# Expert retrieval by row gathers, replaced by dense products over all experts with a gate table in DRAM

## The chip, the cores and the metric

The kernel runs on one core of a Trainium2 chip. The metric is the device time of one execution in microseconds. Everything is fp32.

## What is computed

The reference is one decoder layer on 1024 tokens of width 1024: attention of two kinds, an output projection, then a channel mixer that retrieves experts. The change is in the mixer:

```python
s1, s2 = q[:, :, 0] . keys1, q[:, :, 1] . keys2      # per token, 8 heads, 128 keys on each side
v1, i1 = top_k(s1, 16);  v2, i2 = top_k(s2, 16)
top_s, pos = top_k(all 256 sums v1 + v2, 16)
idx  = i1 * 128 + i2 of those 16                     # one of 16384 experts
gate = softmax(top_s)
h    = gelu(x2[token] . u[idx])                      # u, v: 16384 x 1024
out[token] = x1[token] + sum over 8 x 16 picks of gate * h * v[idx]
```

So each token uses 128 of the 16384 rows of u and of v. A last rmsnorm with a gain follows.

## The kernel before

The 1024 tokens are 8 tiles of 128, one token to a partition. The stages run one after another with barriers between: `project`, `stick`, `window` and `mix` (attention, output projection; `mix` leaves x1 and the normed x2 in DRAM and x2 transposed in SBUF as `x2_t`), then `experts`.

`experts` begins with the key scores (class `KeyScores`, L796 to L894). A unit is one of 16 half-heads by some tiles: 8 matmuls give the queries (L874), ScalarE copies them (L847), one matmul of 128 columns a tile gives the scores (L884), ScalarE copies those out (L856). The first pass does tiles 0 and 1 (16 units of 256 columns), the second tiles 2 to 7 (32 units, of 512 and 256 columns in turn). Scores go to DRAM.

Routing runs on VectorE (L1103 to L1189): two rounds of the eight largest on each half-head, a table of 256 sums a head, two rounds again, then a comparison with a ramp that looks up the keys' numbers. Every step waits for the one before. ScalarE does the exponential (L1316).

Then, for each tile, 128 picks in groups of 8. GpSimd issues for every pick one gather of 128 rows of 4 KB, one for each token, from u or from v (L1063):

```python
nc.gpsimd.indirect_dma_start(
    out=ring[:, k, :], out_offset=None, in_=table,
    in_offset=bass.IndirectOffsetOnAxis(ap=stage[:, half, k:k + 1], axis=0)).then_inc(full[k], 16)
```

VectorE multiplies the gathered rows of u with x2 and sums (L1197). The gelu is put together from an exponential on ScalarE and small VectorE operations (`weigh`). ScalarE turns each pick's weight into a diagonal matrix (L1335), and TensorE adds diagonal times gathered rows of v in PSUM, two matmuls of 512 columns a pick (L1372). The gathers of v of tile t and of u of tile t+1 alternate on GpSimd's queue, each behind a ring of 8 buffers. In the last tile VectorE takes one pick of eight from TensorE (`extra`, L1221). `finish` (L1233) adds x1, norms and hands the tile to SP's queue.

What sets the order is written out by hand: each engine runs its own program, and semaphores with counts tie them. SP's queue carries loads and stores that are not gathers, in program order, and a wait in it holds up what is behind it.

## Time and profile before

| | us |
|---|---|
| median of 3 runs | 4058.27 (4055.64 to 4059.77) |
| span of the profiled execution | 4053.9 |
| TensorE busy (matmul) | 2946.8 (73%) |
| VectorE busy | 2097.3 (52%) |
| ScalarE busy | 704.7 (17%) |
| GpSimd busy | 2393.8 (59%) |
| DMA, mean over the span | 1153.17 MB, 284 GB/s |

The profile is of one execution; its span runs from the first instruction to the last, and the execution times of the runs include what lies around it. An engine's busy share is an average over stages that have different limits, so it has to be read by stretches. In a group of instructions the first number behind the bar is the time in which at least one of them ran, the second the mean duration of one; matmuls are pipelined, so their durations overlap.

### The profile page before, as it was taken

Reading aid. Unit: us, or ns where it says so; the run is one execution under the profiler, and the core shown is the slowest. Engines: PE = TensorE matmul, PEld = TensorE weight load, DVE = VectorE, ACT = ScalarE, POOL = GpSimd, SP = SyncE. Lnnn points to the kernel's source line nnn. Section 1 sums busy time; section 2 is a strip of 40 time slices with the busy share of each in tenths; the row PEclk is TensorE's granted clock in tenths of the full one; section 3 lists DMA queues with packets and bytes.
Section 4 is the critical chain, followed back from the end, with each engine's and each line's share of the span. In section 5 each row is a group of like instructions: output and inputs, shape, how many; then the busy total and the mean of one; then the engine's idle time right before and its main releaser. Section 6 shows DMA issues by size and latency. Waiting matters only on the chain.

```text
span 4053.9 us, 36202 instructions
## 1 busy us (share of the span) xinstructions
PE 2946.8 (73%) x8280; PEld 1429.7 (35%) x8280; DVE 2097.3 (52%) x4538; ACT 704.7 (17%) x1566; POOL 2393.8 (59%) x2391
## 2 busy tenths in 40 slices
PE   8998978899056776666666676666766667666699
PEld 4655564566022232222222232222322223222243
DVE  1007872258856555654665465556645654444411
ACT  1116632111011111111111111111111111111122
POOL 1001004116777777777777777777777777777765
PEclk8999999999577888778887887878888788888899
DMA  3000012558899999999999999999999999999998
GB/s 104 32 0 1 1 47 85 166 167 298 286 369 324 358 370 348 347 348 360 354 357 346 370 345 348 353 374 334 353 351 381 335 343 356 365 354 356 354 334 304
DMA packets 352122, 1153.17 MB, mean 284 GB/s; under 512 B 36240, under 2 KB 80272, under 8 KB 351120
## 3 DMA queue, kind: packets, MB, share of 16 engines
q0 software_dynamic: 294912, 1073.87, 71.6%
q1 hardware_dynamic: 57104, 78.14, 5.6%
q8 instruction: 36, 0.59, 0.1%
q14 instruction: 70, 0.57, 0.0%
HBM read 1130.90 MB, written 20.97 MB: 284 GB/s over the span
## 4 chain that ended last, share of the span: by engine, by line
issue 27%; POOL 27%; PE 12%; DVE 8%; DMA 6%; POOLq 2%; DVEq 0%; ACT 0%; another core or an unknown queue 0%; SPq 0%; ACTq 0%
POOL ex_u L1063 14%; POOL ex_v L1063 11%; PE ex_acc L1372 10%; DMA ex_u<-in_peer_u,ex_index_u 4%; DMA ex_v<-in_peer_v,ex_index_v 2%; DVE ex_prod L1197 2%; PE kl_q L874 2%; DVE bias L1197 1%; POOL ex_index_v L1055 1%; DVE ex_left L1115 1%; DVE ex_half_i L1114 1%; POOLq L993 1%; DVE ex_half_v L1111 1%; POOLq L994 1%; POOL ex_index_u L1055 0%
## 5 line engine op out<-in xcount | busy, mean ns | idle before, releaser
L1372 PE MATMUL ex_acc<-ex_v,ex_diag 128*128 128x512 f32 x4032 | 2017.0, 664 | 1007.4 <-DMA ex_v<-in_peer_v,ex_index_v 768.5
L1372 PEld LDWEIGHTS ex_acc<-ex_v,ex_diag 128*128 128x128 f32 x4032 | 854.8, 215 | 2168.9 <-issue 2160.9
L1063 POOL DMA_INDIRECT ex_u<-in_peer_u,ex_index_u x1024 | 1114.3, 1088 | 385.4 <-issue 318.5
L1063 POOL DMA_INDIRECT ex_v<-in_peer_v,ex_index_v x1024 | 1066.7, 1042 | 414.5 <-issue 306.2
L1197 DVE CUSTOM_DVE_ANT_0 ex_prod<-ex_u,ex_x 128x1024 f32<-128x1024 f32 x512 | 628.7, 1228 | 1008.7 <-DMA ex_u<-in_peer_u,ex_index_u 878.2
L1335 ACT ACTIVATE ex_diag<-ident,ex_wt 128x128 f32<-128x128 f32 x1008 | 398.1, 401 | 2242.4 <-PE ex_acc L1372 1517.9
L1197 DVE CUSTOM_DVE_ANT_0 bias<-ex_u,ex_x 128x1024 f32<-128x1024 f32 x512 | 628.8, 1228 | 80.6 <-DMA ex_u<-in_peer_u,ex_index_u 53.2
L874 PE MATMUL kl_q<-x_t,ex_v 128*128 128x256 f32 (+1 forms) x768 | 228.3, 450 | 0.8 <-DVE keys_t L1254 0.8
L468 POOL TENSOR_SCALAR_AFFINE_SELECT st_sp<-st_sp 128x1024 f32<-128x1024 f32 x8 | 8.7, 1090 | 362.4 <-DVE st_sp L422 362.4
L252 PE MATMUL pj_acc<-x_t,pj_w 128*128 128x512 f32 x384 | 167.4, 599 | 1.3 <-DVE x_t L207 1.3
L874 PEld LDWEIGHTS kl_q<-x_t,ex_v 128*128 128x128 f32 x768 | 142.3, 190 | 66.4 <-issue 53.6
L415 DVE SCALAR_TENSOR_TENSOR x_t<-st_zs 128x1024 f32<-128x1024 f32 x36 | 45.4, 1262 | 142.6 <-ACT st_zs L371 142.4
L775 PE MATMUL mx_y<-qk_t,mx_mt 128*128 128x512 f32 x256 | 114.4, 605 | 3.7 <-ACT mx_mt L706 3.7
L252 PEld LDWEIGHTS pj_acc<-x_t,pj_w 128*128 128x128 f32 x384 | 73.7, 192 | 94.0 <-issue 92.3
L754 POOL TENSOR_TENSOR mx_hs<-mx_hs,minus_half 128x16 f32<-128x16 f32 x8 | 23.2, 2905 | 137.3 <-DMA mx_g<-in_norm_g 131.1
L325 PE MATMUL st_c<-st_sp,tri 128*128 128x512 f32 x144 | 79.4, 644 | 9.3 <-POOL st_sp L468 8.1
L1197 DVE DVE_READ_ACCUMULATOR2_ANT ex_dots<- 128x1 f32 x1024 | 84.1, 82 | 0.0
L1068 POOL TENSOR_TENSOR ex_index_ut<-ex_index,ex_zero_i 128x128 int32<-128x128 int32 x8 | 7.8, 979 | 126.7 <-DVEq L1189 124.3
L224 DVE COPY pj_w_twice<-pj_w 128x1024 f32<-128x1024 f32 x2 | 1.3, 690 | 145.9 <-DMA pj_w<-in_w_in 145.9
L775 PEld LDWEIGHTS mx_y<-qk_t,mx_mt 128*128 128x128 f32 x256 | 48.9, 194 | 64.5 <-issue 58.8
L249 PE MATMUL pj_acc<-pj_w,x_t 128*128 128x256 f32 (+1 forms) x384 | 69.9, 344 | 0.0
L1055 POOL TENSOR_TENSOR ex_index_v<-ex_index_vt,ex_zero_i 128x8 int32<-128x8 int32 x128 | 60.2, 470 | 11.9 <-PE ex_acc L1372 5.7
(162 smaller groups left out, 1930.2 us busy)
## 6 DMA issues: line engine op xcount, KB each, us to landing
ex_v<-in_peer_w_q SPq DMA_DIRECT2D x16, 1024.0 KB, 5.8
ex_u<-in_peer_u,ex_index_u POOLq DMA_INDIRECT x1024
ex_v<-in_peer_v,ex_index_v POOLq DMA_INDIRECT x1024
pj_w<-in_w_in SPq DMA_DIRECT2D x9, 1024.0 KB, 5.8
x_scratch<-mx_x SPq DMA_DIRECT2D x16, 512.0 KB, 2.7
ex_x<-x_scratch SPq DMA_DIRECT2D x16, 512.0 KB
ex_sc<-score_scratch SPq DMA_DIRECT2D x7, 1024.0 KB
mixed<-in_x SPq DMA_DIRECT2D x8, 512.0 KB, 4.1
```

Of the source, the lines that this page charges most:

```text
L249: last = nc.tensor.matmul(acc[:, n % 4, 0:at[1]], h_t[:, c, part * P:(part + 1) * P], slot[:, c, at[0]:at[0] + at[1]], **st)
L252: last = nc.tensor.matmul(acc[:, n % 4, :], slot[:, c, at:at + P], h_t[:, c, part * HALF:(part + 1) * HALF], **st)
L325: last = nc.tensor.matmul(csum[:, cols], tri[:], soft[:, n % 3, cols], start=True, stop=kb == i)
L415: nc.vector.scalar_tensor_tensor(out=lsp[:, n % 2, :], in0=zs[:, n % 4, :], scalar=-1.0, in1=zs[:, n % 4, :], op0=ALU.mult, op1=ALU.max).t ...
L775: last = nc.tensor.matmul(y[:, t % 2, hf * HALF:(hf + 1) * HALF], m_t[:, t % 2, c, :], w[:, c, hf * HALF:(hf + 1) * HALF], start=c == 0, s ...
L874: last = self.nc.tensor.matmul(self.q[:, n % 2, 0:tiles * P], self.w[:, g % self.ring, c, (b % 2) * P:(b % 2 + 1) * P], self.x2_t[:, c, fi ...
L993: engine.wait_ge(signal, value)
L1055: nc.gpsimd.tensor_tensor(stage[:, half, :], tile_index[:, bass.ds(j * RG, RG)], zero_i[:, 0:RG], ALU.add).then_inc(ready, 1)
L1063: nc.gpsimd.indirect_dma_start(out=ring[:, k, :], out_offset=None, in_=table, in_offset=bass.IndirectOffsetOnAxis(ap=stage[:, half, k:k + ...
L1197: nc.vector.tensor_tensor_reduce(out=prod[k % 2][:], in0=u[:, k, :], in1=x2[:], scale=1.0, scalar=0.0, op0=ALU.mult, op1=ALU.add, accum_ou ...
L1335: nc.scalar.activation(diag[:, k, :], ident[:], ACT.Copy, scale=wt[:, bass.ds(j * RG + k, 1)]).then_inc(diag_ready, 1)
L1372: ins = nc.tensor.matmul(acc[:, hf * HALF:(hf + 1) * HALF], diag[:, k, :], v[:, k, hf * HALF:(hf + 1) * HALF], start=first and k == 0, sto ...
```

## The change

`experts` is rewritten; the stages before it stay, but for `mix`, which no longer stores x2. Nothing is gathered. The 16384 experts are 128 chunks of 128. The tiles form three teams, [0, 1], [2, 3, 4] and [5, 6, 7], and each team passes over all chunks. For one chunk and one team (an iteration, 384 in all):

- SP loads the chunk of u (laid out transposed on the host, 512 KB) and of v (512 KB), each into a ring of 4 (`load_u`, `load_v`).
- TensorE: `hidden(k)`, 8 matmuls with the team's columns of `x2_t` as the moving side, gives expert x token products in the PSUM bank `hp`.
- ScalarE: `gelu(k)` with the built-in function. VectorE: `gated(k)` multiplies with the chunk's gates.
- TensorE: `values(k)` multiplies with v and adds in PSUM, for each tile of the team two matmuls of 512 columns.

The gates of a tile are a table of 128 chunks x 128 experts x 128 tokens that is zero but for the picks. It is made in 32 batches of 4 tokens: VectorE makes two one-hot matrices, picks by keys (`one_hots`), one of them weighted with the gates; TensorE multiplies them, one matmul of 128 columns a token (`build`), into the PSUM bank `gp`; ScalarE copies it with a turn of the axes (`read_gates`) to a staging buffer, and after 32 tokens SP stores 2 MB to DRAM (`store_gates`). SP loads them back in blocks of 8 chunks (`load_gates`). Both move in runs of 1 KB.

Tiles 0 and 1 are routed and their tables made before the loop. For tiles 2 to 7 the routing, cut into 61 pieces, and the batches are spread over the iterations of team 0 and team 1 by the tables `ROUTES`, `TURNS` and `BUILDS`; team 2 has neither. All loops are unrolled.

The core of the diff:

```diff
+CHUNKS = 128
+TEAMS = [[0, 1], [2, 3, 4], [5, 6, 7]]
+RING = 4
+SUB = 32
+BATCH = 4
+BLOCK = 8
...
+    ROUTES = {0: [(2, 0, 3), (3, 21, 2), (4, 53, 2), (5, 86, 2)], 1: [(6, 0, 2), (7, 32, 2)], 2: []}
+    TURNS = {0: {22: 2, 56: 3, 90: 4, 125: 5}, 1: {33: 6, 67: 7}, 2: {}}
+    BUILDS = {0: [(2, 24), (3, 58), (4, 92)], 1: [(5, 0), (6, 35), (7, 69)], 2: []}
+    PIECES = 61
...
+                def load_u(k):
+                    if k >= RING:
+                        sp.wait_ge(h_ready, k - RING + 1)
+                    sp.dma_start(u[:, k % RING, :, :], peer_ut[k % CHUNKS]).then_inc(u_in[k % RING], 16)
+                def load_v(k):
+                    if k >= RING:
+                        sp.wait_ge(v_done, k - RING + 1)
+                    sp.dma_start(v[:, k % RING, :], v_view[k % CHUNKS]).then_inc(v_in[k % RING], 16)
+                def load_gates(n):
+                    team = TEAMS[n // BLOCKS]
+                    if n >= 2:
+                        sp.wait_ge(a_ready, BLOCK * (n - 1))
+                    if n % BLOCKS == 0:
+                        for s in range(2):
+                            sp.wait_ge(gates_stored[s], 16 * (SUBS // 2) * (team[-1] + 1))
+                    subs = len(team) * SUBS
+                    sp.dma_start(gb[:, n % 2, 0:subs, :],
+                                 gate_dram[team[0] * SUBS:team[0] * SUBS + subs, n % BLOCKS].rearrange(
+                                     "s p f -> p s f")).then_inc(gb_in[n % 2], 16)
+                def store_gates(t, q):
+                    s = t * SUBS + q
+                    sp.wait_ge(gp_read, first_use(t) + 1 + (q + 1) * SUB // BATCH)
+                    sp.dma_start(gate_dram[s].rearrange("k p f -> p k f"),
+                                 stage[:, s % 2, :, :].rearrange("p (k c) t -> p k (c t)", c=BLOCK)).then_inc(
+                                     gates_stored[s % 2], 16)
...
+                for k in range(RING):
+                    load_u(k)
+                    load_v(k)
+                for n in range(UNITS):
                     ks.store(sp, n)
-                    if n == SIDES + 8:
+                    if n == SIDES + 12:
                         load_scores(1)
                 ks.all_stored(sp)
-                load_scores(2)
-                load_x2(1)
-                with sp.Fori(1, TILES - 2) as t:
-                    load_scores(t + 2)
-                    load_x2(t + 1)
-                    turn_over(t)
-                load_x2(TILES - 1)
-                turn_over(TILES - 2)
-                turn_over(TILES - 1)
-                sp.wait_ge(y_done, TILES)
-                sp.dma_start(out_v[TILES - 1], y[:]).then_inc(stored, 16)
+                sp.wait_ge(ks.s_ready, UNITS)
+                for t in TEAMS[0]:
+                    for q in range(SUBS):
+                        store_gates(t, q)
+                    if t == 0:
+                        load_scores(2)
+                load_gates(0)
+                load_gates(1)
+                for k in range(TOTAL):
+                    l, c = k // CHUNKS, k % CHUNKS
+                    if k + RING < TOTAL:
+                        load_u(k + RING)
+                    if RING <= k + RING - 1 < TOTAL:
+                        load_v(k + RING - 1)
+                    if c % BLOCK == 2 and c > BLOCK and c // BLOCK + 1 < BLOCKS:
+                        load_gates(l * BLOCKS + c // BLOCK + 1)
+                    if k >= 1 and (done := built_at(k - 1)) and (done[1] + 1) % (SUB // BATCH) == 0:
+                        store_gates(done[0], done[1] // (SUB // BATCH))
+                    for t, first, rate in ROUTES[l]:
+                        if c == first + 20 // rate + 3 and t + 1 < TILES:
+                            load_scores(t + 1)
+                    if l >= 1:
+                        for j, t in enumerate(TEAMS[l - 1]):
+                            if c == j + 8:
+                                store_out(t, j)
+                    if c == 60:
+                        load_x1(l)
+                    if c == CHUNKS - 1 and l + 1 < len(TEAMS):
+                        load_gates((l + 1) * BLOCKS)
+                        load_gates((l + 1) * BLOCKS + 1)
...
+                def one_hots(t, i):
+                    b = t * (P // BATCH) + i
+                    if i == 0:
+                        dve.wait_ge(gp_read, first_use(t) + 1)
+                    if b >= 2:
+                        dve.wait_ge(gp_full, first_use((b - 2) // (P // BATCH)) + 2 + (b - 2) % (P // BATCH))
+                    cols = slice(i * BATCH, (i + 1) * BATCH)
+                    nc.vector.tensor_tensor(oh[:, b % 2, 0, :, :], bcast(iota[:].unsqueeze(1), [P, BATCH, NK]),
+                                            bcast(tr[:, t % 2, 1, cols].unsqueeze(2), [P, BATCH, NK]), ALU.is_equal)
+                    for j in range(BATCH):
+                        n = i * BATCH + j
+                        last = nc.vector.tensor_scalar(oh[:, b % 2, 1, j, :], iota[:], tr[:, t % 2, 0, n:n + 1],
+                                                       tr[:, t % 2, 2, n:n + 1], ALU.is_equal, ALU.mult)
+                    last.then_inc(oh_ready, 1)
+                def gated(k):
+                    team, c = team_of(k), k % CHUNKS
+                    block = k // BLOCK
+                    subs, width = len(team) * SUBS, len(team) * P
+                    dve.wait_ge(gelu_done, k + 1)
+                    dve.wait_ge(gb_in[block % 2], 16 * (block // 2 + 1))
+                    if k >= 2:
+                        dve.wait_ge(v_done, k - 1)
+                    at = c % BLOCK * SUB
+                    nc.vector.tensor_tensor(a[:, k % 2, 0:width].rearrange("p (s t) -> p s t", t=SUB),
+                                            act_h[:, k % 2, 0:width].rearrange("p (s t) -> p s t", t=SUB),
+                                            gb[:, block % 2, 0:subs, at:at + SUB], ALU.mult).then_inc(a_ready, 1)
...
+                gated(0)
+                for k in range(TOTAL):
+                    l, c = k // CHUNKS, k % CHUNKS
+                    if l >= 1:
+                        if c == 0:
+                            for j in range(len(TEAMS[l - 1])):
+                                add_rows(l - 1, j)
+                    if k + 1 < TOTAL:
+                        gated(k + 1)
+                    if l >= 1:
+                        for j, t in enumerate(TEAMS[l - 1]):
+                            if c == j + 3:
+                                mean(t)
+                            if c == j + 5:
+                                scale_rows(t, j)
+                    if k + 1 < TOTAL and (batch := built_at(k + 1)):
+                        one_hots(*batch)
+                    if what := routed_at(k):
+                        for n in range(what[1], what[2]):
+                            route(what[0], n)
+                l = len(TEAMS) - 1
+                for j in range(len(TEAMS[l])):
+                    add_rows(l, j)
+                for t in TEAMS[l]:
+                    mean(t)
+                for j, t in enumerate(TEAMS[l]):
+                    scale_rows(t, j)
...
+                def read_gates(t, i):
+                    s = t * SUBS + i * BATCH // SUB
+                    act.wait_ge(gp_full, first_use(t) + 2 + i)
+                    if i * BATCH % SUB == 0 and s >= 2:
+                        act.wait_ge(gates_stored[s % 2], 16 * (s // 2))
+                    at = i * BATCH % SUB
+                    nc.scalar.activation(stage[:, s % 2, :, at:at + BATCH], gp[:].rearrange("p t n -> p n t"),
+                                         ACT.Copy).then_inc(gp_read, 1)
+                def gelu(k):
+                    width = len(team_of(k)) * P
+                    act.wait_ge(h_ready, k + 1)
+                    if k >= 2:
+                        act.wait_ge(a_ready, k - 1)
+                    nc.scalar.activation(act_h[:, k % 2, 0:width], hp[:, 0:width], ACT.Gelu_apprx_tanh).then_inc(gelu_done, 1)
...
+                def build(t, i):
+                    b = t * (P // BATCH) + i
+                    pe.wait_ge(oh_ready, b + 1)
+                    pe.wait_ge(gp_read, first_use(t) + 1 + i)
+                    for j in range(BATCH):
+                        last = nc.tensor.matmul(gp[:, j, :], oh[:, b % 2, 0, j, :], oh[:, b % 2, 1, j, :], start=True, stop=True)
+                    last.then_inc(gp_full, 1)
+                def hidden(k):
+                    team = team_of(k)
+                    first, width = team[0] * P, len(team) * P
+                    pe.wait_ge(u_in[k % RING], 16 * (k // RING + 1))
+                    if k >= 1:
+                        pe.wait_ge(gelu_done, k)
+                    for j in range(CH):
+                        last = nc.tensor.matmul(hp[:, 0:width], u[:, k % RING, j, :], x2_t[:, j, first:first + width],
+                                                start=j == 0, stop=j == CH - 1)
+                    last.then_inc(h_ready, 1)
...
+                def values(k):
+                    team, c = team_of(k), k % CHUNKS
+                    pe.wait_ge(v_in[k % RING], 16 * (k // RING + 1))
+                    pe.wait_ge(a_ready, k + 1)
+                    for j, t in enumerate(team):
+                        if c == 0 and k >= 1 and j < len(team_of(k - 1)):
+                            pe.wait_ge(y_ready, team_of(k - 1)[j] + 1)
                         for hf in range(2):
+                            last = nc.tensor.matmul(acc[:, j, hf * HALF:(hf + 1) * HALF], a[:, k % 2, j * P:(j + 1) * P],
+                                                    v[:, k % RING, hf * HALF:(hf + 1) * HALF],
+                                                    start=c == 0, stop=c == CHUNKS - 1)
+                    last.then_inc(v_done, 1)
...
+                for t in TEAMS[0]:
+                    turn_picks(t)
+                    for i in range(P // BATCH):
+                        build(t, i)
+                hidden(0)
+                pe.wait_ge(ks.s_read, UNITS)
+                for k in range(TOTAL):
+                    if k + 1 < TOTAL:
+                        hidden(k + 1)
+                    if (t := turned_at(k)) is not None:
+                        turn_picks(t)
+                    values(k)
+                    if batch := built_at(k):
+                        build(*batch)
...
+        if name == "peer_u":
+            a = _np.ascontiguousarray(a.reshape(CHUNKS, P, CH, P).transpose(0, 3, 2, 1))
```

`route` does what the old `pick_` functions did, piece by piece. `add_rows`, `mean` and `scale_rows` finish a tile; GpSimd only takes the power of the mean square. The ring of w_q in the key scoring has 3 slots where it had 4 (they lie in `gb` now), and the exponential of tile 0 is asked of ScalarE behind unit 26, where it was behind unit 18.

## Rows read from the trace of the kernel before

**Rows 1.** The stretches: us, then busy time of each engine, clock, DMA share, GB/s
```profile
core 0: us, PE busy (x) PEld busy (x) DVE busy (x) ACT busy (x) POOL busy (x), PEclk, DMA share, GB/s
...
0.00:770.00 770.00, 680.33 (x3225) 400.37 (x3225) 304.14 (x378) 245.66 (x398) 99.80 (x71) 0.95 0.13 45
770.00:1020.00 250.00, 249.47 (x1024) 174.49 (x1024) 161.28 (x538) 44.15 (x112) 85.24 (x75) 1.00 0.70 235
1020.00:4054.00 3034.00, 2016.97 (x4032) 854.80 (x4032) 1631.91 (x3624) 414.92 (x1057) 2208.75 (x2246) 0.82 0.94 349
```

**Rows 2.** The page, part 3: DMA queues (packets, MB, share of 16 engines)
```profile
q0 software_dynamic: 294912, 1073.87, 71.6%
q1 hardware_dynamic: 57104, 78.14, 5.6%
```

**Rows 3.** Groups by line and form: busy, mean ns | idle before, releasers
```profile
L1372 PE MATMUL ex_acc<-ex_v,ex_diag 128*128 128x512 f32 x4032 | 2017.0, 664 | 1007.4 <-DMA ex_v<-in_peer_v,ex_index_v 768.5 <-ACT ex_diag L1335 142.6 <-issue 96.2
...
L1063 POOL DMA_INDIRECT ex_u<-in_peer_u,ex_index_u x1024 | 1114.3, 1088 | 385.4 <-issue 318.5 <-POOL ex_index_u L1055 60.8 <-DVE ex_dots L1197 4.0
...
L874 PE MATMUL kl_q<-x_t,ex_v 128*128 128x256 f32 x512 | 115.7, 379 | 0.8 <-DVE keys_t L1254 0.8
```

**Rows 4.** TensorE in order of time, key scoring: start, us, line, operands
```profile
777.43 3.62 PE L874 MATMUL kl_q<-x_t,ex_v 128*128 128x256 f32 x16
780.89 0.61 PE L884 MATMUL kl_s<-keys_t,kl_qt 128*128 128x128 f32 x4
...
832.03 7.03 PE L874 MATMUL kl_q<-x_t,ex_v 128*128 128x512 f32 x16
838.90 0.61 PE L884 MATMUL kl_s<-keys_t,kl_qt 128*128 128x128 f32 x4
...
842.80 1.05 PE L884 MATMUL kl_s<-keys_t,kl_qt 128*128 128x128 f32 x8
843.69 6.60 PE L874 MATMUL kl_q<-x_t,ex_v 128*128 128x512 f32 x15
```

**Rows 5.** TensorE in order of time, the last tile
```profile
3848.80 195.49 PE L1372 MATMUL ex_acc<-ex_v,ex_diag 128*128 128x512 f32 x448 [15.95 <-ACT ex_diag L1335]
```

**Rows 6.** Two stretches, TensorE alone: us, busy, clock, DMA share, GB/s
```profile
3000.00:3500.00 500.00, 333.49 (x656) 0.82 0.95 356
3850.00:4044.00 194.00, 194.00 (x447) 0.99 0.92 333
```

**Rows 7.** Groups by form, ScalarE, VectorE and GpSimd
```profile
L856 ACT ACTIVATE kl_out<-kl_s 128x512 f32<-128x512 f32 x16 | 9.6, 597 | 8.3 <-PE kl_s L884 6.3 <-issue 2.0
...
L1129 DVE TENSOR_TENSOR ex_cand<-ex_half_v 128x256 f32<-128x256 f32 x64 | 22.3, 420 | 1.7 <-DVE ex_half_f L1127 0.8
...
L759 POOL TENSOR_TENSOR mx_rs<-mx_rs,minus_half 128x1 f32<-128x1 f32 x8 | 4.4, 556 | 55.4 <-DVE mx_rs L741 55.4
```

**Rows 8.** VectorE in order of time, routing of tile 0
```profile
849.66 2.04 DVE L1140 MAX8 ex_best<-ex_cand 128x8 f32<-128x256 f32 x6
...
864.66 0.23 DVE L1156 TENSOR_SCALAR ex_part_i<-ex_pos 128x128 uint32<-128x128 uint32 x1
...
883.10 0.29 DVE L1186 TENSOR_TENSOR ex_gates<-ex_gate_e,ex_gsum 128x128 f32<-128x128 f32 x1
```

**Rows 9.** ScalarE in order of time, end of key scoring
```profile
1019.55 0.87 ACT L856 ACTIVATE kl_out<-kl_s 128x512 f32<-128x512 f32 x2 [0.51 <-PE kl_s L884]
```

**Rows 10.** DMA issues: KB each, median us to landing
```profile
ex_v<-in_peer_w_q SPq DMA_DIRECT2D x16, 1024.0 KB, 5.8
...
x_scratch<-mx_x SPq DMA_DIRECT2D x16, 512.0 KB, 2.7
```

**Rows 11.** Everything in order of time, the end
```profile
4044.38 1.23 DVE L1239 TENSOR_TENSOR ex_y<-ex_acc,bias 128x1024 f32<-128x1024 f32 x1 [2.12 <-PE ex_acc L1372]
4045.64 1.03 ACT L1324 ACTIVATE ex_ysq<-ex_y 128x1024 f32<-128x1024 f32 x1 [12.83 <-DVE ex_y L1239]
...
4050.87 0.34 SPq L1040 DMA_DIRECT2D out<-ex_y  x1
```

More of the change, by code:

```diff
@@ L893, in multiply, with experts, team_of, built_at @@
             self.score(pe, n)
-def experts(nc, sem, ident, spare, keys_t, keys1, keys2, w_q, x2_t, score_dram, x1_dram, x2_dram, peer_u, peer_v, final_g, out):
-    RG = 8
-    GROUPS = PICKS // RG
+def experts(nc, sem, ident, minus_half, keys_t, keys1, keys2, w_q, x2_t, score_dram, gate_dram, x1_dram, peer_ut, peer_v,
+            final_g, out):
     score_t = score_dram.rearrange("(t p) n -> t p n", p=P)
     x1_v = x1_dram.rearrange("(t p) n -> t p n", p=P)
-    x2_v = x2_dram.rearrange("(t p) n -> t p n", p=P)
     out_v = out.rearrange("(t p) n -> t p n", p=P)
+    v_view = peer_v.rearrange("(c p) d -> c p d", p=P)
+    TOTAL = len(TEAMS) * CHUNKS
+    SUBS = P // SUB
+    USES = P // BATCH + 1
+    BLOCKS = CHUNKS // BLOCK
+    MOST = max(len(team) for team in TEAMS)
+    ROUTES = {0: [(2, 0, 3), (3, 21, 2), (4, 53, 2), (5, 86, 2)], 1: [(6, 0, 2), (7, 32, 2)], 2: []}
+    TURNS = {0: {22: 2, 56: 3, 90: 4, 125: 5}, 1: {33: 6, 67: 7}, 2: {}}
+    BUILDS = {0: [(2, 24), (3, 58), (4, 92)], 1: [(5, 0), (6, 35), (7, 69)], 2: []}
+    PIECES = 61
+    def team_of(k):
+        return TEAMS[k // CHUNKS]
+    def built_at(k):
+        for t, first in BUILDS[k // CHUNKS]:
+            if first <= k % CHUNKS < first + P // BATCH:
+                return t, k % CHUNKS - first
+        return None
+    def turned_at(k):
+        return TURNS[k // CHUNKS].get(k % CHUNKS)
+    def routed_at(k):
+        for t, first, rate in ROUTES[k // CHUNKS]:
+            n = (k % CHUNKS - first) * rate
+            if 0 <= n < PIECES:
+                return t, n, min(PIECES, n + rate)
+        return None
     with ExitStack() as ctx:
@@ L1067, in copy_index @@
-                def copy_index(dest, source, value):
-                    nc.gpsimd.tensor_tensor(dest[:], source[:], zero_i[:], ALU.add).then_inc(index_moved, 1)
-                    hold(pool, index_moved, value)
-                pool.wait_ge(picked, 1)
-                copy_index(index_ut, index, 1)
-                with pool.Fori(0, GROUPS // 2) as pair:
-                    for half in range(2):
-                        gathers(0, 2 * pair + half, half, peer_u, u, index_ut, index_u, u_full, u_free, iu_ready)
@@ L1086, in _ @@
-                copy_index(index_vt, index_ut, 2 * TILES)
-                with pool.Fori(0, GROUPS // 2) as pair:
-                    for half in range(2):
-                        gathers(TILES - 1, 2 * pair + half, half, peer_v, v, index_vt, index_v, v_full, v_free, iv_ready,
-                                RG - 1)
+                nc.gpsimd.iota(iota_i[:], pattern=[[1, NK]], base=0, channel_multiplier=0).then_inc(setup, 1)
+                for t in range(TILES):
+                    pool.wait_ge(mean_done, t + 1)
+                    nc.gpsimd.tensor_tensor(fs[:, 2, t:t + 1], fs[:, 1, t:t + 1], minus_half[:, 0:1],
+                                            ALU.pow).then_inc(rstd_done, 1)
@@ new lines, in _ @@
+                gelu(0)
+                for k in range(TOTAL):
+                    l, c = k // CHUNKS, k % CHUNKS
+                    if k + 1 < TOTAL:
+                        gelu(k + 1)
+                    if (t := turned_at(k)) is not None:
+                        read_turned(t)
+                    if batch := built_at(k):
+                        read_gates(*batch)
+                    for t, first, rate in ROUTES[l]:
+                        if c == first + 39 // rate + 2:
+                            gate_exp(t)
+                    if l >= 1:
+                        for j, t in enumerate(TEAMS[l - 1]):
+                            if c == j + 1:
+                                square(t, j)
@@ L1364, in _ @@
+                for j, t in enumerate(TEAMS[-1]):
+                    square(t, j)
             @block.tensor
             def _(pe):
-                def group(t, j, first, last, slots):
-                    at = t * PICKS + j * slots
-                    for k in range(slots):
-                        pe.wait_ge(v_full[k], 16 * (t * GROUPS + j + 1))
-                        pe.wait_ge(diag_ready, at + k + 1)
-                        for hf in range(2):
-                            ins = nc.tensor.matmul(acc[:, hf * HALF:(hf + 1) * HALF], diag[:, k, :],
-                                                   v[:, k, hf * HALF:(hf + 1) * HALF],
-                                                   start=first and k == 0, stop=last and k == slots - 1)
-                        ins.then_inc(v_free, 1)
@@ L1377, in tile, with turn_picks @@
-                def tile(t, slots=RG):
-                    group(t, 0, True, False, slots)
-                    with pe.Fori(1, GROUPS - 1) as j:
-                        group(t, j, False, False, slots)
-                    group(t, GROUPS - 1, False, True, slots)
+                def turn_picks(t):
+                    pe.wait_ge(picked, t + 1)
+                    if t >= 1:
+                        pe.wait_ge(gp_read, first_use(t))
+                    for j in range(3):
+                        last = nc.tensor.transpose(gp[:, j, :], row[:, j, :], ident[:])
+                    last.then_inc(gp_full, 1)
```

549 lines of the change are left out of this document (201 added, 348 removed).

## The prediction, made before the changed kernel had run

> **What bounds the kernel now.** Read the stretches first [rows 1]: 770 us of attention and mixing, 250 us of key scoring with TensorE full at 249.5 us, then 3034 us of experts. In the last, the 16 DMA engines are busy 0.94 of the time at 349 GB/s, TensorE 2017 of 3034 us, VectorE 1632. The DMA table [rows 2] names the traffic: 1073.87 MB of gathered rows of u and v. The groups by line [rows 3] show who waits for it: TensorE's 4032 records of L1372 sat idle 1007 us, 769 of them for a gather of v. GpSimd is close behind: 1.09 us for a gather of u [rows 3], those of v alike, 2209 us busy in the stretch [rows 1]. So the expert stage is a DMA stage with a third of TensorE free. The last row of [rows 3] settles how a matmul is to be counted: 32 units of 8 matmuls of 256 columns stand as x512. Each fp32 matmul of the program is two records. A 512-column record takes 195.49/448 = 0.436 us in a dense run [rows 5], so a matmul takes about twice that.
>
> **What goes.** All gathers, GpSimd's work, the 1024 products of 1.23 us on VectorE, the diagonals on ScalarE, 16 stores of x2 and 8 loads of it: the DMA bound ends. In return every token meets every one of 16384 experts.
>
> **TensorE's new work, the term that decides.** Key scoring already runs the three shapes, back to back with full cover [rows 4]. Eight matmuls of 256 columns: 780.89-777.43 = 3.46 us. Eight of 512: 838.90-832.03 = 6.87 us, or 0.859 each. Four of 128: 843.69-842.80 = 0.89 us. Eight of 384, by interpolation between the first two: 5.165 us (the cost is linear in columns, 1.68 ns each).
> - A team of two tiles, one chunk of 128 experts: `hidden` is 8x256, 3.46 us; `values` is 4x512, 3.44 us; 6.90 us. Times 128: 883 us.
> - A team of three: 8x384 is 5.165, 6x512 is 5.15; 10.32 us. Times 256 for two teams: 2641 us.
> - Gate tables of tiles 2 to 7, inside the loop: 6x32 batches of 4 matmuls of 128 columns, 0.89 us: 171 us. Six turns of 3 transposes: 4 us.
> Sum of the loop: 3699 us of TensorE that nothing hides, since it is TensorE itself, against the 3034 us of the whole old stage. The old stage used 2016 matmuls there, the new one 6144 times two shapes; trading 1 us of gather for dense products costs more products than DMA gave back.
>
> **What lies beside it.** Each iteration is 7.8 us (team of two with a batch) to 11.2 us.
> - ScalarE: the gelu from PSUM, 256 or 384 columns, up to the 0.60 us of 512 columns [rows 7], and the read of four gate tables, 512 columns, 0.60 us. 1.2 of 7.8. The single `hp` buffer makes `hidden(k+1)` wait for `gelu(k)`, but `values(k-1)`, 3.4 us, stands between.
> - VectorE: `gated`, 384 columns at the 1.2 ns a column of the 1024-column sum (1.23 us in [rows 11]), 0.46. One-hots of a batch: a 512-column compare, 0.70 (twice 22.3/64 [rows 7]), and four of 128 columns at 0.23 [rows 8], 0.9. Routing: 37 pieces of tile 0 took 849.66 to 883.39 [rows 8], 0.92 us each; two or three an iteration, 1.8 to 2.8. At most 4.8 of 7.8 us. The three-piece rate stands only where no batch does.
> - DMA: u and v, 1.05 MB a chunk, at the gathers' rate (1073.87 MB in 0.716 of 4054 us [rows 2], 370 KB/us) 2.8 us. Gates move in runs of 1 KB as w_q does, 1 MB in 5.8 us [rows 10]: 0.13 MB read and 0.25 MB written a chunk, 2.1 us. 4.9 of 7.8 us, and issued four chunks ahead. SP's waits in this loop are all for things already past; the gate loads at a team's first chunk are the tightest and I give them 2 us each, 4 us.
> All of it is hidden; its worth is nothing as long as TensorE is behind it in no iteration.
>
> **Before the loop.** Attention, mixing and scoring stay: ScalarE's last copy of scores ends at 1020.4 [rows 9]. (x2's last store fell at the end of mixing, 1 us at most, left out; the scoring ring of 3 instead of 4 is reloaded in 5.8 us [rows 10] against 7.8 us a group.) Tile 0 is routed by 883 as before [rows 8] or some 10 us later, as its exponential is now asked of ScalarE at unit 26; tile 1's 61 pieces end before 1020 except the last three, which wait for ScalarE's second exponential behind the last unit. Some 4 us for these, the transposes and the first one-hots: 1024. Then 64 batches with one PSUM bank: weights and four matmuls 1.05 [rows 4], plus 0.2, the read 0.60 [rows 7], two handshakes of 0.1 (estimate; the chain of score matmul, copy and next matmul shows no more): 2.0 us, 128 us. From below it is 1.65 (table and read alone), from above 3.0 if ScalarE's write with a stride of 128 bytes takes double; I take 2.0. With tile 1's turn, 2.5 us, the last table is read at 1154.5. Then comes what nothing covers: the last 2 MB store, some 9.6 us (2 MB at 3.8 us per MB and 2 us of latency, from 5.8 us for 1 MB and 2.7 for half [rows 10]), the load of the first gates, 5.8, and `gated`, 0.5. `values(0)` starts at about 1170.5, with `hidden(0)` and `hidden(1)`, 6.9 us of the loop, already done.
> The Trainium skill (DMA: Bandwidth & Descriptors, section Anatomy of one DMA — SWDGE (gpsimd) path) fits a transfer with 2.0 us plus bytes over 436 GB/s: an estimate of 6.8 us for the store, and the sum would be 3 us less; w_q's 5.8 us a megabyte, where the fit gives 4.4, is why I don't take it.
>
> **After the loop.** The last team's tail: three sums of 1.23 us, a square of 1.03 [rows 11], GpSimd's power 0.56 [rows 7], three scalings of 1.28, and the store's 2.7 [rows 10]: 12.3 us with the small steps.
>
> **The sum.** 1170.5 + (3699 - 6.9) + 4 + 12.3 = 4879 us of span. Against its own: the profiled execution spans 4053.9, the median of the runs is 4058.3, so 4.4 us lie around a span. 4883 us, 20% slower.
>
> **The rivals.**
> - A cover fails where batches run. Mechanism: in the 192 iterations with a batch, TensorE waits at `build` or at `values` for VectorE, whose queue holds `gated` behind one-hots and routing. It decides where VectorE needs over 7.8 us; for it speaks that each piece waits for the one before and that VectorE is a strict line; against it 4.8 of 7.8. At 1 us each: 192 us more, 5075.
> - The clock falls. In the stretch where TensorE waited a third of the time the granted clock was 0.82, in the dense last tile 0.99 [rows 6], in scoring 1.00 [rows 1]. Levels are 1.2 and 2.4 GHz, so 0.82 is a mix of both. The loop has no waits of that kind; if it ran at 0.82 nonetheless, 3699/0.82 is 812 us more, 5695.
> - The other side: matmuls in a sustained run come closer together than in scoring. To be no slower than before, the loop must lose 825 of 3699 us: a 512-column matmul under 0.67 us. For it speaks only that the old stage was rarely dense; against it, the one dense run of 448 records, with weights changed at each, held 0.436 us, and in scoring 8x512 held 0.859 a matmul with nothing to wait for. Halved cost per record, for a bound, gives 4883-1850 = 3033.
> The Trainium skill (TensorE: Matmul & The Clock Gate, section Back-to-back issue gap) gives a sustained 131 ns per matmul of 512 columns, and FP8 and Floating Point Precision (section TensorE Precision Notes) four passes for true fp32. As an estimate that is 0.52 us a matmul, a loop of about 2260 us, and 3440 us in all: faster than before. By that rule the old kernel's last tile would show 0.26 us a record; the trace shows 0.436.
>
> **How the numbers follow.** The forecast (TensorE-bound, 4835 to 4960) has 0.80; a failing cover, 0.14; the clock, 0.03; faster, 0.02; 0.01 for a change within 0.2%, about what can be told from none. The low end is 4835: batches at 1.65 us (-22) and shapes a percent cheaper (-26). The high end takes in batches at 3.0 us (+64) and half a microsecond lost in each of 192 iterations (+96): 5040. Faster 0.02, same 0.01, slower 0.97.
>
> **What would show it.** Right: TensorE busy over 95% from about 1170 to 4865 with clock 0.99 or 1.00; chunks of 6.9, 7.8, 10.3 and 11.2 us; teams ending near 2135, 3545 and 4866; GpSimd idle; DMA share under 0.65; `hidden` and `values` idle before them only a few us, and 15 us idle at the start of `values`. Wrong: idle time before `values` charged to VectorE's product or to a gate load; a gate-table group of much over 0.89 us; a first `values` well off 1170; a mean record of 512 columns away from 0.43 us.

## The result and the profile after

The changed kernel takes 4938.4 us in the median of four executions (4937.3 without the one named below), the kernel before 4059.0: ratio 1.216, 95% interval 1.214 to 1.218. The forecast was 4883. One of four executions took 11387 us at a mean granted clock of 0.458 (one of the two-bank version took 18093 us); it is left out of every comparison and its cause stays open.

From the page of the kernel after, which answers to [rows 1, 2]: busy time, the granted clock in 40 slices, the one data queue, and the chain that ended last by engine.

```profile
PE 4763.4 (97%) x16560; PEld 2813.4 (57%) x16560; DVE 1389.9 (28%) x3922; ACT 649.2 (13%) x1195; POOL 106.2 (2%) x78
...
PEclk9999899965999999999999999999999999999999
...
q1 hardware_dynamic: 297744, 606.67, 37.5%
...
PE 83%; ACT 1%; DVE 0%; DMA 0%; issue 0%; DVEq 0%; SPq 0%; ACTq 0%
```

TensorE is busy 97% of the span and is 83% of the chain. The clock stands at 8 or 9 tenths in every slice but two, just before the loop. The queue takes 37.5% of the engines' span where gathers took 71.6 [rows 2]. By stretches (us, busy of TensorE, its weight loads, VectorE, ScalarE, GpSimd, clock, DMA share, GB/s):

```profile
770.00:1022.00 252.00, 251.04 (x1034) 175.89 (x1033) 106.16 (x451) 44.80 (x114) 0.00 (x0) 1.00 0.37 117
1022.00:1035.00 13.00, 0.00 (x0) 0.00 (x0) 12.59 (x22) 0.53 (x2) 0.00 (x0) 0.58 0.10 30
1035.00:1218.00 183.00, 131.46 (x514) 114.34 (x515) 108.26 (x316) 38.12 (x64) 0.00 (x0) 0.50 0.26 86
1218.00:1233.00 15.00, 9.47 (x36) 7.49 (x35) 0.58 (x2) 2.65 (x4) 0.00 (x0) 0.84 0.76 247
1233.00:4924.00 3691.00, 3690.68 (x11762) 2113.77 (x11762) 852.44 (x2751) 313.82 (x608) 3.79 (x5) 1.00 0.44 143
```

The last line is the loop: 3691 us of which TensorE is busy 3690.7, at clock 1.00, beside a DMA share of 0.44. The third is the 64 batches before it, at 0.50. The groups of the three new products, with VectorE's gating and one-hots, where [rows 3] stood:

```profile
L1382 PE MATMUL ex_hp<-x_t,ex_u 128*128 128x384 f32 (+1 forms) x6144 | 1828.1, 451 | 0.6 <-ACT ex_act_h L1321 0.6
L1394 PE MATMUL ex_acc<-ex_v,ex_a 128*128 128x512 f32 x4096 | 1823.3, 593 | 5.0 <-DVE ex_a L1235 5.0
...
L1235 DVE TENSOR_TENSOR ex_a<-ex_act_h,ex_gb 128x384 f32<-128x384 f32 (+1 forms) x384 | 197.4, 514 | 2840.5 <-ACT ex_act_h L1321 2796.2
...
L1372 PE MATMUL ex_gp<-ex_oh 128*128 128x128 f32 x2048 | 333.6, 315 | 63.9 <-ACT ex_stage L1313 48.3
...
L1222 DVE TENSOR_SCALAR ex_oh<-ex_iota,ex_tr 128x128 f32<-128x128 f32 x1024 | 284.4, 342 | 0.0
```

The two big ones show 5.6 us idle together, and all of it falls before the loop's first `values` at 1233.0. Both have two records a matmul: 384 x 8 x 2 = 6144, and 8 tiles x 128 x 2 x 2 = 4096. In order of time, where team 0 becomes team 1:

```profile
2110.18 1.05 PE L1372 MATMUL ex_gp<-ex_oh 128*128 128x128 f32 x8
2111.07 3.62 PE L1382 MATMUL ex_hp<-x_t,ex_u 128*128 128x256 f32 x16
2114.53 3.60 PE L1394 MATMUL ex_acc<-ex_v,ex_a 128*128 128x512 f32 x8
2117.96 1.05 PE L1372 MATMUL ex_gp<-ex_oh 128*128 128x128 f32 x8
...
2202.90 5.32 PE L1382 MATMUL ex_hp<-x_t,ex_u 128*128 128x384 f32 x16
2208.06 5.31 PE L1394 MATMUL ex_acc<-ex_v,ex_a 128*128 128x512 f32 x12
2213.21 1.05 PE L1372 MATMUL ex_gp<-ex_oh 128*128 128x128 f32 x8
```

From 2110.18 to 2117.96 an iteration of team 0 with a batch takes 7.78 us (predicted 7.8). `hidden` and `values` take 3.46 and 3.43, a batch 0.89, as in [rows 4]. In team 1 `hidden` takes 5.16, `values` 5.15, and the iteration with a batch 11.20 (2202.90 to 2214.10, predicted 11.2).

### The profile page after: what moved, and what is told of

It is laid out like the page before. It is cut to its first block, busy times and chain, and to the rows that moved or that the text cites. A ratio compares the mean times of both kernels' runs of the same rounds, so it can differ in the third digit from the quotient of the medians.

```text
span 4935.5 us, 41804 instructions
## 1 busy us (share of the span) xinstructions
PE 4763.4 (97%) x16560; PEld 2813.4 (57%) x16560; DVE 1389.9 (28%) x3922; ACT 649.2 (13%) x1195; POOL 106.2 (2%) x78
## 3 DMA queue, kind: packets, MB, share of 16 engines
q1 hardware_dynamic: 297744, 606.67, 37.5%
## 4 chain that ended last, share of the span: by engine, by line
PE 83%; ACT 1%; DVE 0%; DMA 0%; issue 0%; DVEq 0%; SPq 0%; ACTq 0%
PE ex_acc L1394 36%; PE ex_hp L1382 36%; PE ex_gp L1372 6%; PE ex_acc L870 4%; ACT ex_stage L1313 1%; PE ex_acc L880 1%; DMA gate_scratch<-ex_stage 0%; DMA ex_gb<-gate_scratch 0%; DMA ex_oh<-in_peer_keys 0%; DVE ex_row L1197 0%; PE ex_acc L1404 0%; ACT ex_junk L1327 0%; PE ex_gp L1364 0%; DVE ex_cand L1191 0%; DVE ex_cand L1185 0%
## 5 line engine op out<-in xcount | busy, mean ns | idle before, releaser
L1382 PE MATMUL ex_hp<-x_t,ex_u 128*128 128x384 f32 (+1 forms) x6144 | 1828.1, 451 | 0.6 <-ACT ex_act_h L1321 0.6
L1394 PE MATMUL ex_acc<-ex_v,ex_a 128*128 128x512 f32 x4096 | 1823.3, 593 | 5.0 <-DVE ex_a L1235 5.0
L1382 PEld LDWEIGHTS ex_hp<-x_t,ex_u 128*128 128x128 f32 x6144 | 1154.0, 190 | 613.7 <-issue 92.1
L1394 PEld LDWEIGHTS ex_acc<-ex_v,ex_a 128*128 128x128 f32 x4096 | 778.8, 190 | 877.1 <-issue 803.6
L1235 DVE TENSOR_TENSOR ex_a<-ex_act_h,ex_gb 128x384 f32<-128x384 f32 (+1 forms) x384 | 197.4, 514 | 2840.5 <-ACT ex_act_h L1321 2796.2
L1372 PEld LDWEIGHTS ex_gp<-ex_oh 128*128 128x128 f32 x2048 | 315.7, 226 | 172.9 <-issue 155.1
L1372 PE MATMUL ex_gp<-ex_oh 128*128 128x128 f32 x2048 | 333.6, 315 | 63.9 <-ACT ex_stage L1313 48.3
L1222 DVE TENSOR_SCALAR ex_oh<-ex_iota,ex_tr 128x128 f32<-128x128 f32 x1024 | 284.4, 342 | 0.0
L870 PE MATMUL ex_acc<-x_t,ex_gb 128*128 128x256 f32 (+1 forms) x768 | 228.3, 450 | 0.8 <-DVE keys_t L1259 0.8
L1218 DVE TENSOR_TENSOR ex_oh<-ex_iota,ex_tr 128x512 f32<-128x512 f32 x256 | 175.8, 687 | 71.4 <-PE ex_gp L1372 65.3
```

Of the source, the lines that this page charges most:

```text
L870: last = self.nc.tensor.matmul(self.q[:, n % 2, 0:tiles * P], self.w[:, g % self.ring, c, (b % 2) * P:(b % 2 + 1) * P], self.x2_t[:, c, fi ...
L1218: nc.vector.tensor_tensor(oh[:, b % 2, 0, :, :], bcast(iota[:].unsqueeze(1), [P, BATCH, NK]), bcast(tr[:, t % 2, 1, cols].unsqueeze(2), [P ...
L1222: last = nc.vector.tensor_scalar(oh[:, b % 2, 1, j, :], iota[:], tr[:, t % 2, 0, n:n + 1], tr[:, t % 2, 2, n:n + 1], ALU.is_equal, ALU.mult)
L1235: nc.vector.tensor_tensor(a[:, k % 2, 0:width].rearrange("p (s t) -> p s t", t=SUB), act_h[:, k % 2, 0:width].rearrange("p (s t) -> p s t" ...
L1372: last = nc.tensor.matmul(gp[:, j, :], oh[:, b % 2, 0, j, :], oh[:, b % 2, 1, j, :], start=True, stop=True)
L1382: last = nc.tensor.matmul(hp[:, 0:width], u[:, k % RING, j, :], x2_t[:, j, first:first + width], start=j == 0, stop=j == CH - 1)
```

## Experiments

All times are medians beside runs of the kernel before on the same chip, which took 4024 us (for e1 to e4), 4016 (e5 to e7) and 4068 (e8 and e9). The dense kernel without loads (e3) took 4936 where the old one took 4024, and the changed one 4937 where the old took 4059: the old kernel's time differs with the chip, that of the version bound by TensorE hardly does. So the dense versions are compared by their spans.

**What costs the loop its time: no load of u and v behind the first four (e3).** TensorE's waits for them, which this cut of the diff leaves out, ask only for a slot's first load.

```diff
-                    if k + RING < TOTAL:
-                        load_u(k + RING)
-                    if RING <= k + RING - 1 < TOTAL:
-                        load_v(k + RING - 1)
...
```

> Leaves out every load of u and v but the first four chunks, whose data are used again and again. Theory (TensorE alone bounds the loop and all transfers are hidden): span 4935, within 5 us. Rival (transfers cost the loop something here and there): over 20 us shorter.

4936.2 us, span 4936.6 against 4935.5. The loop by itself:

```profile
1180.00:4900.00 3720.00, 3703.49 (x11842) 2133.94 (x11843) 873.53 (x2814) 323.25 (x624) 3.64 (x5) 0.99 0.11 37
```

The same stretch of the changed kernel has TensorE busy 3704.4 us at a DMA share of 0.44. The share falls to 0.11 and nothing else moves: the loads of u and v were hidden, and the rival falls. The gate tables' transfers stay in this run; that they cost nothing is read from the loop of the changed kernel, in which TensorE is never idle.

**Half of the product with v (e4).**

```diff
-                        for hf in range(2):
+                        for hf in range(2 if c in (0, CHUNKS - 1) else 1):
```

> Leaves out the second 512 output columns of the product with v in 126 of 128 chunks of each team: 8 x 126 = 1008 matmuls of 512 columns fewer. Theory (each costs its 0.859 us in full): 866 us shorter, span 4070, about the time of the kernel before. Rival (something else, VectorE or the transfers, soon takes over as the bound): less than 700 us shorter, with waits for it before TensorE's products.

4073.1 us, span 4070.1: 865 us less, 0.859 us for each of the 1008 matmuls left out. TensorE in order of time in team 1:

```profile
3003.59 5.32 PE L1382 MATMUL ex_hp<-x_t,ex_u 128*128 128x384 f32 x16
3008.74 2.74 PE L1394 MATMUL ex_acc<-ex_v,ex_a 128*128 128x512 f32 x6
3011.32 5.32 PE L1382 MATMUL ex_hp<-x_t,ex_u 128*128 128x384 f32 x16
```

`values` takes 2.58 us instead of 5.15, and `hidden` follows without a gap: at 7.74 us an iteration nothing else is late yet. That kernel, with 23% of its loop gone, is still not faster than the old one.

**The same question of the old kernel: half of its product with gathered v (e7).**

```diff
-                        for hf in range(2):
+                        for hf in range(1):
                             ins = nc.tensor.matmul(acc[:, hf * HALF:(hf + 1) * HALF], diag[:, k, :],
```

> The kernel before, with the second 512 output columns of the product with gathered v left out, 1008 of its 2016 matmuls. Theory (the old stage is bound by its gathers, at a DMA share of 0.94): under 1% shorter, though the last tile, where TensorE alone ran for 195 us, gives back some 80 us of it: at most 2% shorter. Rival (TensorE's share of the old stage was a bound too, as its 2017 us suggest): 5% or more shorter.

4001.5 us, ratio 0.996 (0.994 to 0.997). TensorE's busy time in the expert stage falls by 704 us against [rows 1], the time by 15. That stretch, cut off at 4000 us (us, busy of TensorE, its weight loads, VectorE, ScalarE, GpSimd, clock, DMA share, GB/s):

```profile
1020.00:4000.00 2980.00, 1312.92 (x2042) 412.30 (x2040) 1629.79 (x3629) 416.30 (x1058) 2202.30 (x2249) 0.71 0.96 356
```

So 1008 matmuls were worth 865 us in the new kernel and 15 in the old. The expected 80 us of the last tile did not come. It takes 178 us (3815.7 to 3993.4) where it had taken 195 [rows 5]: TensorE, which had run dense, now waits there 72 times for a gather, 1.9 us at the longest and 38.8 us in all.

The run clears TensorE as the old stage's bound. It does not tell whether the 16 DMA engines (share 0.94) or GpSimd, which issues the gathers (2209 of 3034 us busy), set the gathers' pace. In the chain that ended last in the old kernel GpSimd's own work is 27% of the span, time in which an engine waited for nothing that the profile shows another 27%, and transfers are 6%. No run separates the two; both end with the gathers.

**The 64 batches before the loop: a filler matmul (e1).** They had taken 2.83 us each, not 2.0. In order of time, in the changed kernel:

```profile
1059.90 0.60 ACT L1313 ACTIVATE ex_stage<-ex_gp 128x512 f32<-128x512 f32 x1 [2.23 <-PE ex_gp L1372]
...
1060.64 2.05 PE L1372 MATMUL ex_gp<-ex_oh 128*128 128x128 f32 x8 [0.78 <-ACT ex_stage L1313]
1062.73 0.60 ACT L1313 ACTIVATE ex_stage<-ex_gp 128x512 f32<-128x512 f32 x1 [2.23 <-PE ex_gp L1372]
...
1063.47 2.05 PE L1372 MATMUL ex_gp<-ex_oh 128*128 128x128 f32 x8 [0.78 <-ACT ex_stage L1313]
```

Eight records last 2.05 us; in the loop, from 2110.18, they last 1.05. Then TensorE waits 0.78 us for ScalarE. TensorE began the stage after 13.4 us without work.

```diff
                         build(t, i)
+                        nc.tensor.matmul(hp[:, 0:2 * P], ident[:], x2_t[:, 0, 0:2 * P], start=True, stop=True)
```

> Before the loop one fp32 matmul of 256 columns, whose product nobody reads, follows each of the 64 gate-table batches, where TensorE idles 0.78 us waiting for ScalarE. The changed kernel takes 2.83 us a batch there at a granted clock of about 0.5. Theory (the clock stays at 1.2 GHz because TensorE pauses in every batch): the clock rises, eight records last 1.05 us instead of 2.05, a batch takes about 1.85 us, and the span falls by 55 to 65 us to some 4875. Rival (a batch is as long as its chain of handshakes, whatever the clock): 2.83 us stays or grows, span 4935 or more.

4878.3 us, span 4880.7: 55 less, for added work. The stretch, whose clock had been 0.50:

```profile
1035.00:1150.00 115.00, 92.18 (x564) 70.37 (x565) 98.90 (x289) 33.92 (x57) 0.00 (x0) 0.95 0.36 119
```

**Two banks instead (e2).**

```diff
+        spare_gp = acc[:, 2, 0:HALF].rearrange("p (t n) -> p t n", n=NK)
+        def bank(t, i):
+            return spare_gp if t in TEAMS[0] and i % 2 else gp[:]
...
-                    pe.wait_ge(gp_read, first_use(t) + 1 + i)
+                    pe.wait_ge(gp_read, first_use(t) + 1 + (max(i - 1, 0) if t in TEAMS[0] else i))
```

> The batches before the loop alternate between two PSUM banks, so that TensorE need not wait for ScalarE's read of the last one; no filler matmul. Theory: the pause goes, TensorE is bound by its own 1.9 us at the low clock or by VectorE's one-hots (0.69 + 1.11 = 1.8 us a batch), the clock rises, VectorE is the bound at 1.8 to 1.9 us: span some 60 us shorter, 4875. Rival (the clock stays low without fillers and each batch keeps 2.05 us): 50 us shorter at most, granted clock of that stretch still about 0.5.

4865.0 us, span 4862.8: 73 less. The batches and the loop:

```profile
1035.00:1146.00 111.00, 78.11 (x516) 66.25 (x517) 105.18 (x322) 38.10 (x64) 0.00 (x0) 0.95 0.42 143
...
1161.00:4851.00 3690.00, 3689.98 (x11762) 2113.35 (x11761) 851.36 (x2749) 313.27 (x608) 3.63 (x5) 1.00 0.43 143
```

The clock is 0.95 without any filler, so the rival falls; the loop is as long as ever. A batch takes 1.63 us:

```profile
1100.75 0.68 DVE L1223 TENSOR_TENSOR ex_oh<-ex_iota,ex_tr 128x512 f32<-128x512 f32 x1
...
1100.89 1.16 PE L1377 MATMUL ex_gp<-ex_oh 128*128 128x128 f32 x8 [0.47 <-DVE ex_oh L1227]
1101.35 1.10 DVE L1227 TENSOR_SCALAR ex_oh<-ex_iota,ex_tr 128x128 f32<-128x128 f32 x4
...
1102.38 0.68 DVE L1223 TENSOR_TENSOR ex_oh<-ex_iota,ex_tr 128x512 f32<-128x512 f32 x1
```

That is VectorE alone, 0.68 + 1.10 less their overlap. My bound for it, 1.8 us, had added two durations whose ends and starts overlap by 0.15 us in all; hence 73 us and not 60.

My theory had the pause go, and it has not: TensorE waits 0.47 us of every 1.63, 29%, for VectorE, at full clock. In the changed kernel it had waited 0.78 of 2.83, 28%, at 0.50. So the share of the pause does not tell the two apart. What does differ is how the stage starts here:

```profile
1037.24 2.08 PE L1377 MATMUL ex_gp<-ex_oh 128*128 128x128 f32 x8 [13.35 <-DVE ex_oh L1227]
1039.12 1.91 PE L1377 MATMUL ex_acc<-ex_oh 128*128 128x128 f32 x8
...
1043.00 1.09 PE L1377 MATMUL ex_acc<-ex_oh 128*128 128x128 f32 x8
1045.01 1.16 PE L1377 MATMUL ex_gp<-ex_oh 128*128 128x128 f32 x8 [0.92 <-DVE ex_oh L1227]
```

The first three batches run back to back at the lower clock, the clock rises in the fourth, and the pauses begin only then. With the filler (e1) it is the same: no gap until the clock has risen, then a pause of 0.34 us in every 1.91. In the changed kernel TensorE pauses from the first batch on, and the clock rises only at about 1222, in `hidden(0)`, which follows the last batch without a gap. That an uninterrupted start brings the clock up fits all three traces. Whether a pause of 0.78 us would take it down again was not tried.

**A second buffer for the turned picks (e6, with the two banks).** In the changed kernel VectorE stood 50.8 us idle, until TensorE had turned tile 0's picks behind the last score; then the rest of tile 1's routing ran alone:

```profile
1021.93 2.48 DVE L1197 TENSOR_REDUCE ex_row<-ex_cand 128x64 f32<-128x1024 f32 x2 [50.79 <-PE ex_gp L1364]
...
1030.01 2.47 DVE L1197 TENSOR_REDUCE ex_row<-ex_cand 128x64 f32<-128x1024 f32 x2
...
1035.18 2.07 PE L1372 MATMUL ex_gp<-ex_oh 128*128 128x128 f32 x8 [13.36 <-DVE ex_oh L1222]
```

```diff
-        row = sb("ex_row", [P, 3, PICKS])
+        rows = sb("ex_row", [P, 2, 3, PICKS])
...
-                            if side == 0 and k == 5 and t >= 1:
-                                dve.wait_ge(gp_full, first_use(t - 1) + 1)
+                            if side == 0 and k == 5 and t >= 2:
+                                dve.wait_ge(gp_full, first_use(t - 2) + 1)
```

> As with two banks before the loop, and the turned picks have a second buffer, so that tile 1's last 12 routing pieces, which stood idle 51 us behind the transposes of tile 0 and then took 11 us, run under the key scoring. Theory (these 11 us are on the path): 11 us under the two-bank kernel's 4865, so 4854. Rival (the second exponential behind the last scoring unit sets the start): same 4865.

4852.1 us against 4865.0, span 4847.9 against 4862.8. What is left between the last scores and the first batch is the exponential and five small steps:

```profile
1019.44 0.31 ACT L1304 ACTIVATE ex_gate_e<-ex_gate_e 128x128 f32<-128x128 f32 x1
...
1022.51 1.78 PEld L1377 LDWEIGHTS ex_gp<-ex_oh 128*128 128x128 f32 x8 [3.32 <-DVE ex_oh L1227]
```

This is the best fp32 dense version here, and still 21% slower than the old kernel.

**One record a matmul: bfloat16 operands (e5).** This keeps e6's edits; the rings of u and v have 3 slots.

```diff
+        ub = sb("ex_ub", [P, 2, CH, NK], BF)
+        vb = sb("ex_vb", [P, 2, D], BF)
...
+                    nc.gpsimd.tensor_copy(vb[:, k % 2, :], v[:, k % RING, :]).then_inc(vc, 1)
...
+                    nc.scalar.activation(ub[:, k % 2, :, :], u[:, k % RING, :, :], ACT.Copy).then_inc(uc, 1)
...
-                        last = nc.tensor.matmul(hp[:, 0:width], u[:, k % RING, j, :], x2_t[:, j, first:first + width],
+                        last = nc.tensor.matmul(hp[:, 0:width], ub[:, k % 2, j, :], xb[:, j, 0:width],
```

> The products with u and v run on bfloat16 operands: ScalarE casts each chunk of u and the team's x2, GpSimd each chunk of v, VectorE writes the gated values as bfloat16; rings of 3 for the loads. Routing, scores, gate tables and sums stay fp32. It also has the two banks before the loop and a second buffer for the turned picks. Theory (the dense version loses by the two records of two cycles a column that an fp32 product costs): a product takes one record of 0.216 us per 512 columns, a chunk of a team of three 2.6 us instead of 10.3; then VectorE (gated, one-hots and routing, 4.5 to 5 us an iteration while tables are made) and the transfers (2.8 us for u and v, 1.1 for gates) are the bound, 4 to 5 us an iteration: 2800 to 3200 us in all. Rival (TensorE's time is not what the loop costs, or casting takes its place at over 8 us a chunk): over 4000 us.

2661.3 us, ratio 0.662 (0.661 to 0.664) to the kernel before: faster than both, and than the 2800 I had expected at best: I had put 4 to 5 us on an iteration, and team 0 takes 4.2, team 2 3.4. It rounds the operands of the mixer's two products, which the fp32 kernels do not. TensorE in order of time, where nothing holds it up:

```profile
2201.34 1.46 PE L1428 MATMUL ex_hp<-bias,ex_ub 128*128 128x384 bf16 x8
2202.64 1.46 PE L1440 MATMUL ex_acc<-ex_vb,ex_a 128*128 128x512 bf16 x6
2203.94 1.46 PE L1428 MATMUL ex_hp<-bias,ex_ub 128*128 128x384 bf16 x8
```

`hidden` on 384 columns takes 1.30 us from start to start, `values` another 1.30, and an iteration lasts 2.60 where fp32 took 10.31, a quarter. x8 and x6 are now one record a matmul. The three teams (us, busy of TensorE, its loads, VectorE, ScalarE, GpSimd, clock, DMA, GB/s):

```profile
1160.00:1693.00 533.00, 369.12 (x2277) 245.88 (x2276) 487.82 (x1494) 233.31 (x364) 142.13 (x125) 0.93 0.93 336
1693.00:2225.00 532.00, 464.80 (x2565) 269.73 (x2566) 381.77 (x1076) 245.54 (x364) 149.37 (x130) 0.95 0.98 355
2225.00:2658.00 433.00, 362.27 (x1779) 179.79 (x1777) 92.82 (x138) 188.76 (x259) 135.73 (x130) 0.92 0.97 363
```

**Is it the transfers now (e8)?** The bfloat16 kernel, without the loads of u and v behind the first three chunks.

> The bfloat16 kernel, leaving out every load of u and v but the first three chunks. In it the DMA share is 0.93 to 0.99 from 1150 us on, VectorE is busy 429 of 450 us in team 0. Theory (once a product is one record, transfers bound the last team and VectorE the first, and TensorE neither): the last team loses a third or more of its time, the first nearly nothing, 2350 to 2520 us in all. Rival (TensorE, at 83% busy over the span, is still the bound): within 50 us of 2661.

2500.1 us. The teams:

```profile
1160.00:1687.00 527.00, 359.09 (x2251) 238.52 (x2287) 499.75 (x1503) 230.86 (x365) 140.56 (x126) 0.95 0.28 91
1687.00:2157.00 470.00, 439.01 (x2520) 263.28 (x2562) 375.47 (x1077) 241.79 (x364) 151.49 (x130) 0.99 0.37 117
2157.00:2492.00 335.00, 329.60 (x1751) 173.91 (x1781) 80.53 (x139) 184.80 (x261) 136.05 (x130) 1.00 0.24 76
```

Team 0 is 6 us shorter, bound by VectorE (500 of 527 us busy). Team 1 is 62 us shorter. Team 2 goes from 433 to 335 us: transfers had bound it. Its gain is 23% and not the expected third, because the theory had left out what stands right behind the transfers there: 128 x 2.60 = 333 us of TensorE's own time.

**Gate tables in bfloat16, in blocks of 16 chunks (e9).**

```diff
-BLOCK = 8
+BLOCK = 16
...
-        stage = sb("ex_stage", [P, 2, CHUNKS, SUB])
+        stage = sb("ex_stage", [P, 2, CHUNKS, SUB], BF)
```

> The bfloat16 kernel with gate tables in bfloat16 as well, moved in blocks of 16 chunks, so that a run is 1 KB still: 67 MB instead of 134; rings of 4 again. Theory (transfers bound it where VectorE does not): gates were some 360 us of the transfers' time in the loop, half goes, of which the team bound by VectorE gives nothing: 60 to 160 us shorter, 2500 to 2600. Rival (the loads of u and v alone set the pace): under 30 us.

2536.1 us, ratio 0.6235 (0.622 to 0.625), the fastest here that does all the work. Against e5 that is 125 us less, but its rings of 4 came with it, so they are not the tables' alone.

```profile
1160.00:1679.00 519.00, 354.31 (x2219) 240.18 (x2256) 487.89 (x1460) 227.07 (x359) 138.78 (x123) 0.95 0.84 301
1679.00:2152.00 473.00, 438.54 (x2525) 263.35 (x2566) 375.00 (x1075) 244.46 (x366) 152.47 (x130) 0.99 0.94 345
2152.00:2521.00 369.00, 340.13 (x1744) 175.32 (x1776) 86.88 (x139) 183.89 (x257) 135.41 (x129) 0.96 1.00 390
```

Team 2 still runs at a DMA share of 1.00 and takes 369 us, 34 more than without loads; team 0 is VectorE's as before.

## Why the prediction was right

The sign, the size and the range held; the span came 56 us over the 4879 of the sum. By its terms:

- *The loop on TensorE* was 3692 and 4 for the hand-over of gates; it took 3690.7, from 1233.0 to 4923.7. The three shapes timed in key scoring hold in a run of 3.7 ms, and e4 gives the price of a matmul as 0.859 us, the prediction's own. (Its sentence on "6144 times two shapes" counts records as matmuls: `hidden` is 3072 matmuls, `values` 2048. The sum did not use it.)
- *What lies beside it* costs nothing: TensorE is not idle once between 1233.0 and 4923.7, so not behind a gate load at the teams' borders either, and e3 takes the loads of u and v away without effect. The 4 us were too many.
- *The batches before the loop* were the mis-sized term: 128 + 2.5 us, measured 183.2. The step that failed is "weights and four matmuls 1.05", which was read in key scoring at full clock. The stage starts after 13.4 us without work and pauses 0.78 us in each batch, and the clock stays at its lower level, 1.2 GHz: 2.05. Both e1 (-55 us) and e2 (-73 us) let the first batches run without a gap, and the clock rises. My clock rival had only asked about the loop; the row that showed the danger stood in [rows 6], 0.82 where TensorE waits. The upper bound of 3.0 us a batch held the measured 2.83, but that is luck: it stood there for a slow strided write, which takes 0.60 as in [rows 7].
- *The start of the batches* was put at 1024 and came at 1035.2. I had all but three of tile 1's pieces end under the scoring; the wait for the transposes of tile 0 held twelve back, the three among them. e6 moves the first batch to 1022.5.
- *The first gates*: 16 us predicted, 14.6 from 1218.4 to 1233.0. *The tail*: 12.3 predicted, 11.8, from here to the end of the span at 4935.5:

```profile
4923.71 3.49 DVE L1242 TENSOR_TENSOR ex_xacc<-ex_acc,ex_xacc 128x1024 f32<-128x1024 f32 x3 [9.22 <-PE ex_acc L1394]
```

Two of the prediction's own signs of being wrong came with this: a group of the gate tables well over 0.89 us, and a first `values` at 1233 instead of 1170. They touch the 211 us before the loop and not the reason for the loss. In the range, the low end took 26 us for shapes a percent cheaper; a percent of the whole loop is 37. The result lies too far above it for that to matter.

Of the rivals, a failing cover did not occur. The shorter spacing of products did not either: the estimate of 0.52 us a matmul from the Trainium skill (TensorE: Matmul & The Clock Gate, section Back-to-back issue gap), four passes of 131 ns, stands against 0.859 in e4. The four passes for true fp32 that the Trainium skill gives (FP8 and Floating Point Precision, section TensorE Precision Notes) fit the ratio of 10.31 to 2.60 between fp32 and bfloat16, though the profile shows them as two records.

The reason the change loses is shown from both sides: the same 1008 matmuls are worth 865 us in the new kernel (e4) and 15 in the old (e7). The old expert stage is bound by its gathers and the new loop by TensorE. Behind key scoring the change put 3915 us in the place of 3034: the loop's 3691 us of TensorE alone are 657 more, and the tables before the loop, with the tail, the other 225. With products at a quarter of the price (e5) the same structure is 34% faster than the old kernel.

## What to carry to other kernels

Before trading gathers for dense products, price one iteration on TensorE from a dense stretch of the old trace, counting records per matmul, and hold it against the whole stage that goes; that all other work is hidden gains nothing once TensorE itself is full. Read the clock of the stretch too: a price from a dense stretch need not hold in a chain that starts after a pause and in which TensorE waits for a read in every step; a second bank cured it here. And where the bound is what a data type costs on TensorE, try the type, if its rounding can be borne, before the algorithm is given up.
